# RWKV directions: four elementwise products moved from VectorE to GpSimd between its score factors

## The reference, cut to what matters

```python
a = sigmoid(a0[d] + ad @ a_up[d])
k_d = k * (1.0 + (a - 1.0) * k_a)          # the key of this direction
dirs.append((decay, k_d, a * kk))          # a * kk: rate times key
...
bonus = sum(r * (k_f + k_b) * r_k) * v     # needs the keys of both directions
...
s = s * w_t - (s @ kk_t) ak_t + v_t k_t    # one step of the state, per token
y = s @ r_t
```

## Time and profile before

| | us |
|---|---|
| median of 3 runs | 2219.52 (2217.44 to 2220.51) |
| the profiled execution, its own time | 2221.07 |
| its span | 2219.3 |
| busy TensorE, VectorE, ScalarE, GpSimd | 2041.2, 898.2, 492.2, 103.5 |
| direction 0, rates / decays / scores begin, block ends | 1343.0 / 1359.8 / 1366.7 / 1403 |
| direction 1, the same | 1491.0 / 1508.7 / 1515.6 / 1550 |

### The profile page before, as it was taken

One profiled execution on the slowest core, in us unless ns is written; L12 is line 12 of the kernel. 1 busy time (PEld: TensorE's weight loads), 2 busy tenths in 40 slices (PEclk: granted clock), 3 DMA queues, 4 the chain that ended last, 5 costly groups with the idle time before them and its releaser, 6 DMA issues. The chain is left out here.

```text
span 2219.3 us, 29442 instructions
## 1 busy us (share of the span) xinstructions
PE 2041.2 (92%) x12268; PEld 1209.4 (54%) x12268; DVE 898.2 (40%) x1894; ACT 492.2 (22%) x987; POOL 103.5 (5%) x127
## 2 busy tenths in 40 slices
PE   8999999989999999999998898897977999999994
PEld 3445665536576334585684465783854555544452
DVE  6671064423452112458414677738554221111112
ACT  1000162141122002352023255225212011100001
POOL 0000000002220000000000001302200000000001
PEclk9999999999899999999999998899788999999997
DMA  4222200210001863111121000000027999999995
GB/s 162 76 76 76 76 20 29 68 48 29 29 31 34 341 247 124 57 63 42 39 105 70 26 23 29 2 16 15 2 95 306 414 424 425 424 424 424 424 426 214
DMA packets 54517, 330.35 MB, mean 149 GB/s; under 512 B 6512, under 2 KB 11248, under 8 KB 36080
## 3 DMA queue, kind: packets, MB, share of 16 engines
q1 hardware_dynamic: 53232, 324.26, 37.0%
q0 software_dynamic: 1152, 4.19, 0.5%
HBM read 311.65 MB, written 14.68 MB: 147 GB/s over the span
## 5 line engine op out<-in xcount | busy, mean ns | idle before, releaser
L3514 PE MATMUL psum<-m_ring,m_xg 128*64 128x512 f32 x1024 | 227.9, 600 | 16.9 <-issue 15.8
L246 PE MATMUL psum<-h,wring 128*128 128x512 f32 (+1 forms) x416 | 166.9, 549 | 9.9 <-PEq L93 4.8
L552 PE MATMUL psum<-x,wring 128*128 128x512 f32 x384 | 167.0, 597 | 7.0 <-DVE x L370 7.0
L3514 PEld LDWEIGHTS psum<-m_ring,m_xg 128*64 128x64 f32 x1024 | 77.5, 138 | 164.1 <-issue 162.8
L552 PEld LDWEIGHTS psum<-x,wring 128*128 128x128 f32 x384 | 73.5, 192 | 99.4 <-issue 90.9
L3499 PEld LDWEIGHTS psum<-m_sel,m_htok 128*128 128x128 f32 x1024 | 119.5, 196 | 13.7 <-issue 12.2
L3499 PE MATMUL psum<-m_sel,m_htok 128*128 128x128 f32 x1024 | 123.8, 280 | 1.4 <-DVE m_sel L3490 1.4
L246 PEld LDWEIGHTS psum<-h,wring 128*128 128x128 f32 x416 | 78.3, 195 | 76.8 <-issue 65.0
L3539 PE MATMUL psum<-m_ring,m_hid_t 128*64 128x512 f32 x512 | 115.0, 602 | 0.7 <-ACT m_hid_t L3642 0.7
L3524 DVE TENSOR_TENSOR m_hid<-rstd,psum 64x512 f32<-64x512 f32 x32 | 22.1, 691 | 229.9 <-ACT rstd L3520 229.9
L2056 PE MATMUL psum<-h,wring 128*128 128x512 f32 x192 | 89.5, 623 | 0.9 <-PEq L93 0.7
(11 more groups left out here) (612 smaller groups left out, 3137.3 us busy)
## 6 DMA issues: line engine op xcount, KB each, us to landing
m_ring<-in_w_gate SPq DMA_DIRECT2D x32, 2048.0 KB, 25.7
m_ring<-in_w_up SPq DMA_DIRECT2D x32, 2048.0 KB, 28.0
m_ring<-in_w_down SPq DMA_DIRECT2D x64, 1024.0 KB, 25.5
wring<-in_w1f SPq DMA_DIRECT2D x60, 512.0 KB, 3.3
ada_ring<-in_w_ada SPq DMA_DIRECT2D x12, 2048.0 KB, 10.5
wring<-in_w2f SPq DMA_DIRECT2D x31, 512.0 KB, 3.3
expert_rows<-tmp SPq DMA_DIRECT2D x16, 512.0 KB, 25.9
wring<-in_w1v SPq DMA_DIRECT2D x12, 512.0 KB, 3.2
```

What stands on the lines that cost most here:

```text
L246: return nc.tensor.matmul(place(t, out), lhs, rhs, start=(k == 0), stop=(k == KD - 1))
L552: m = nc.tensor.matmul(K.psum[:, banks[t % 4]], ws.weights(first + t, k), h[:, k], start=(k == 0), stop=(k == KD - 1))
L3514: m = nc.tensor.matmul(K.psum[i * SLOTS:(i + 1) * SLOTS, UP + s], W.xg[:, k, s], w[:, k], start=(k == 0), stop=(k == KD - 1))
```

## The change

Four products per direction go from VectorE to GpSimd. `ak` times `kk` becomes the only GpSimd instruction of the rates (after both halves of `kd`, semaphore `keyed`), so that GpSimd joins the handover `ended`. `bonus` becomes the first GpSimd instruction of the decays and waits for nothing but the handover. `kke` times `kk` is made by GpSimd in two halves of 768 elements, one ahead of its factors of chunk 2 and one ahead of those of chunk 3, and `re` times `r_` (1024 elements) ahead of those of chunk 4. The two products that make `kd` lose their link on VectorE. No transfer is added or moved, and the order of what stays on VectorE, ScalarE and TensorE is the same.

```diff
         for m in range(2):
             eng.wait_ge(sem["sig"], 3 + m)
             link(nc.vector.tensor_scalar(kd[:, m], ak[:, m], -1.0, K.rw[:, 6 + m:7 + m], ALU.add, ALU.mult))
-            link(nc.vector.scalar_tensor_tensor(kd[:, m], kd[:, m], 1.0, k_[:, m], ALU.add, ALU.mult))
-        link(nc.vector.tensor_tensor(ak[:], ak[:], kk[:], ALU.mult))
-        if d == 0:
-            nc.vector.tensor_copy(bonus[:], kd[:, :, CTX:])
-        else:
-            nc.vector.tensor_tensor(bonus[:], bonus[:], kd[:, :, CTX:], ALU.add)
+            nc.vector.scalar_tensor_tensor(kd[:, m], kd[:, m], 1.0, k_[:, m], ALU.add, ALU.mult).then_inc(sem["keyed"], 1)
...
+    def gpsimd(eng, sem):
+        yield 0.6
+        eng.wait_ge(sem["keyed"], 2)
+        nc.gpsimd.tensor_tensor(ak[:], ak[:], kk[:], ALU.mult)
...
-        eng.wait_ge(sem["exped"], 1)
-        nc.vector.tensor_tensor(kke[:], kk[:], kke[:], ALU.mult)
         eng.wait_ge(sem["exped"], 2)
         nc.vector.tensor_tensor(ko[:, 0], kd[:], lw[:], ALU.mult).then_inc(sem["scaled"], 1)
         nc.vector.tensor_tensor(ko[:, 1], ak[:], lw[:], ALU.mult).then_inc(sem["scaled"], 1)
-        eng.wait_ge(sem["exped"], 4)
-        nc.vector.tensor_tensor(re[:], r_[:, :, CTX:], re[:], ALU.mult)
...
     def gpsimd(eng, sem):
+        yield 0.0
+        if d == 0:
+            nc.gpsimd.tensor_copy(bonus[:], kd[:, :, CTX:])
+        else:
+            nc.gpsimd.tensor_tensor(bonus[:], bonus[:], kd[:, :, CTX:], ALU.add)
         yield share
         eng.wait_ge(sem["scaled"], 2)
-        for at_ in scores.engines["gpsimd"](eng, sem):
+        for n, at_ in enumerate(scores.engines["gpsimd"](eng, sem)):
+            if n in (2, 3):
+                m = n - 2
+                eng.wait_ge(sem["exped"], 1)
+                nc.gpsimd.tensor_tensor(kke[:, m], kk[:, m], kke[:, m], ALU.mult)
+            if n == 4:
+                eng.wait_ge(sem["exped"], 4)
+                nc.gpsimd.tensor_tensor(re[:], r_[:, :, CTX:], re[:], ALU.mult)
             yield share + (1 - share) * at_
```

More of the change, by code:

```diff
@@ L2739, in rwkv_direction @@
             (15, rwkv_rates(nc, K, d, up_w, p_mix, kk, k_, kd, ak, lw, ci, ce, e_tot, bias, bonus, range(4))),
-            (54, rwkv_decays(nc, K, kk, r_, kd, ak, lw, ci, ce, at, kke, koT, re, e_tot, range(6),
+            (54, rwkv_decays(nc, K, d, bonus, kk, r_, kd, ak, lw, ci, ce, at, kke, koT, re, e_tot, range(6),
                              rwkv_scores(nc, K, d, r_, kk, kd, ak, both, bias, at, bt, cd, (lw[:], p_mix[:, 4:6]), p_mix[:, 8], range(6)))))
@@ L2811, in vector, with rwkv_decays @@
             nc.vector.tensor_scalar(bias[:, x, :, 2 * NCH:3 * NCH], edge, rate, None, ALU.mult)
-    return Program(["up", "sig", "v"], tensor=tensor, scalar=scalar, vector=vector)
-def rwkv_decays(nc, K, kk, r_, kd, ak, lw, ci, ce, at, kke, koT, re, e_tot, banks, scores):
+    def gpsimd(eng, sem):
+        yield 0.6
+        eng.wait_ge(sem["keyed"], 2)
+        nc.gpsimd.tensor_tensor(ak[:], ak[:], kk[:], ALU.mult)
+    return Program(["up", "sig", "keyed", "v"], tensor=tensor, scalar=scalar, vector=vector, gpsimd=gpsimd)
+def rwkv_decays(nc, K, d, bonus, kk, r_, kd, ak, lw, ci, ce, at, kke, koT, re, e_tot, banks, scores):
     share = 12 / 54
```

## The result

The changed kernel takes 2225.03 us as the median of 12 runs (2220.28 to 2230.53), the kernel before beside it 2218.24 (12 runs): ratio 1.0034 with a 95% interval of 1.0022 to 1.0047, so 7.5 us slower (4.9 to 10.4). One run of the repetition in experiment 8 took 5544.59 us and is left out of its ratio; every other run here lies between 2203 and 2231 us.

What follows compares the result with a forecast made beforehand. The prediction took TensorE as busy for most of the span, with VectorE counting where TensorE waits, in the two RWKV blocks. Rates, decays and scores summed to 4.4 us on the median 2219.5: 2223.9, range 2218.5 to 2229 (forecast's own 2222 to 2226).

Steps and rivals of the forecast that it cites:

- Whole holds: Both blocks: VectorE products with both inputs in SBUF and GpSimd products take turns, whole instruction by whole instruction.
- the turn goes back: Second rival, chance 0.15: VectorE never waits more than 0.54 us within a long GpSimd instruction; about +2 us, 2221.5.
- no contest: Third rival, chance 0.12: a GpSimd product does not hold VectorE up at all; 4.7 us faster, 2214.8.
- Who has the first turn: End of rates and start of decays: GpSimd's start-up of 0.14 us before its first read gives VectorE the turn.
- 1379.3: Score-part collision in direction 0, cited against the first rival: VectorE, started 0.05 us ahead on the same release, went first.
- the first rival: Chance 0.13: GpSimd has the first turn in rates and decays; 3.4 us more, 7.8 us in all, 2227.3.
- rates: Block head up to the handover, with GpSimd's `ak` product: 0.4 us later in direction 0, 0.1 in direction 1.
- decays: Stage after the handover: GpSimd's bonus costs nothing in direction 0; its addition makes L2829 0.5 us later in direction 1.
- Scores: Second half of `kke` and chunk 3's factors delay VectorE's query products: 2.0 us in direction 0, 1.35 in direction 1.
- the ring: Score-part waits: VectorE's mask, ScalarE's corner copy and next query side, VectorE's factors for TensorE; lateness lasts to block end.
- Nothing gained: Taking `kke` and `re` off VectorE gives nothing: VectorE would wait there for an exponential and for TensorE's transposes.
- The sum: 0.4 + 2.0 in direction 0, 0.1 + 0.5 + 1.35 in direction 1: 4.4 us (4.35) slower; forecast chance 0.60.

Runs made afterwards that it cites:

- experiment 8: Kernel before with the bonus alone on GpSimd, behind all factors, where VectorE has only masks left; 2211.34 us, ratio 0.9976, at the repetition 0.9997.
- experiment 2: Kernel before with the bonus alone moved to GpSimd, first in the decays; ratio 0.9991 (0.9975 to 1.0007).
- experiment 3: Kernel before with only `kke` and `re` on GpSimd, between its score factors; 2221.95 us, ratio 1.0017 (1.0006 to 1.0028).
- experiment 7: Changed kernel with the bonus on GpSimd replaced by a memset that reads nothing; VectorE's difference took 1.76 us, no run time given.
- experiment 4: Changed kernel with a small GpSimd memset ahead of the `ak` product and of the bonus; 2218.39 us, ratio 0.9998 to the kernel before.
- experiment 1: Kernel before with only the rate-times-key product (`ak` times `kk`) on GpSimd; 2217.68 us, ratio 0.9995 (0.9985 to 1.0005).

## Why the prediction was right, and what was wrong in it

**Whole holds.** Right. A VectorE product with both inputs in SBUF waits for the rest of a GpSimd product of up to 3.43 us: it was held for 3.25 us, where the forecast's rows showed 0.54. The second and third rivals (the turn goes back, no contest) have fallen. The Trainium skill, "SBUF — State Buffer", section "Who interferes with whom", says that an instruction of VectorE with two SBUF inputs contends with a GpSimd instruction that reads SBUF and not with one that only writes it; the traces agree: products of VectorE took 4.21 us in the changed kernel, 3.96 in experiment 2 and 1.45 in experiment 3, and in experiment 7 one took its bare 1.76.

**Who has the first turn.** This step failed. The forecast said that GpSimd's start-up of 0.14 us keeps it from reading and so gives VectorE the turn. At the four places where it mattered GpSimd's record begins 0.01 to 0.04 us ahead of VectorE's, and GpSimd went first (4.21, 2.62, 4.19 and 3.96 us on VectorE); the 0.59 us after VectorE's end only says how much of a GpSimd product is left once it may read. At 1379.3, which the forecast took as evidence, VectorE's record begins 0.05 us ahead. Where VectorE's instruction before had ended by the time its product started, as at all these places and in experiment 4, the product whose record begins first had the turn.

Where VectorE works without a gap that does not hold. The kernel before, direction 1, and the changed kernel, direction 1:

```profile
1519.96 0.28 DVE L3139 TENSOR_TENSOR p_mix<-r_kk,p_mix 128x128 f32<-128x128 f32 x1
1520.14 1.03 POOL L3179 TENSOR_TENSOR r_lw<-r_kd,p_mix 128x256 f32<-128x256 f32 x1 [2.45 <-ACT p_mix L3097]
1520.16 0.42 DVE L3134 TENSOR_TENSOR r_lw<-r_ak,p_mix 128x256 f32<-128x256 f32 x1
```

```profile
1529.28 1.27 POOL L3187 TENSOR_TENSOR r_lw<-r_kd,p_mix 128x256 f32<-128x256 f32 x1 [2.69 <-ACT p_mix L3105]
1529.34 0.41 DVE L3142 TENSOR_TENSOR r_lw<-r_ak,p_mix 128x256 f32<-128x256 f32 x1
1529.67 0.28 DVE L3143 TENSOR_TENSOR r_lw<-r_ak,p_mix 128x128 f32<-128x128 f32 x1
```

In the first, GpSimd's record begins 0.02 us ahead, and yet L3134, which follows L3139 without a gap, has its bare length, and GpSimd ends 0.59 us behind it. The same stands in the fourteen profiles wherever GpSimd is ahead by 0.02 us or less of a product that follows another VectorE instruction so (37 times). In the second GpSimd is 0.06 to 0.07 us ahead and waits for two products; as far ahead in the second profile of the changed kernel (1380.81) it went first. What decides there is not known. The forecast's reading that GpSimd has its turn between two VectorE instructions that follow without a gap holds for the row that it names (1379.62) and not for these.

What came in place of the forecast's step was the first rival, priced at 3.4 us more. Its parts: rates 0.73 in direction 0 (forecast 0.4, rival 0.8) and 0.05 in direction 1 (0.1, 0.3); decays 0.82 and 2.18 (0 and 0.5; rival 1.0 and 2.3). Experiment 4, which adds two memsets of 0.12 us and so changes the start order, brings the decays to the forecast's figures (0 and 0.5) and the rates to 0.2 and -0.1. The measured 7.5 us are nearer to the rival's 7.8 than to the forecast's 4.35, and the time lies in the range because the range was drawn to hold the rival as well; in that much the forecast was lucky.

**Scores.** The mechanism was right, with the sizes 1.4 to 2.0 in direction 0 (forecast 2.0) and 1.8 to 2.1 in direction 1 (1.35), of which the ring has 1.8 in each. In direction 1 the forecast let chunk 3 meet only one of VectorE's products; both its instructions fell between them, as in direction 0. `re` is covered when the ring is late and costs 1.4 to 1.9 us when it is not (forecast 1.2). The first half of `kke` costs nothing that the ring shows: in direction 0 of experiment 3 it puts the query product of chunk 1 off by 1.6 us, and the first corner copy stands 6.46 us behind the first factor, as before.

**Nothing gained.** Right: with `kke` and `re` gone from VectorE the way to `ko` is 3.31 instead of 3.35 us and the stretch behind it is unchanged (experiment 3).

**The sum.** Rates 0.8, decays 3.0, scores 3.5 or 3.8 (first and second pair of profiles): 7.3 or 7.6 us, against 7.5 measured and 4.35 forecast. Of the 2.9 to 3.3 us that the forecast lacked, some 2.8 are the first turn (rates 0.3, decays 2.5). TensorE's clock added 0.8 us in the first pair of profiles and nothing in the second (-0.1).

**What stays open.** That the whole loss is in the blocks rests on single profiles. The runs of the kernels of experiments 1, 2 and 4 are 1 to 5 us better than their blocks: by their ratios the three parts of the change make -1.1, -2.0 and +3.8 us, together 0.7, where the change makes 7.5, and experiment 4 stands 8 us below the changed kernel, where its blocks account for about 3. Over the 35 runs of the kernel before beside them the time goes with the mean granted clock of the execution, some 1.2 us for 0.001 (correlation -0.61), and these three kernels had 0.9502 to 0.9505 on average against 0.9489, which would be 1.5 to 1.9 us; the runs of the changed kernel and of experiment 3 had 0.9482 and 0.9478, which would be 0.7 and 1.2 us the other way. Why, and whether that is an effect of where the blocks stand in time, was not tried. Nor is it known what makes the transposes of direction 1 meet the lower clock: they did in two of three profiles in which the difference was held for 2.2 us and in none of the eleven others.

## What to carry to other kernels

Before work is moved to GpSimd, look at what VectorE does at the same moment: if it works on two inputs in SBUF, or copies from SBUF to SBUF, the work is not beside it but in line with it, and at half the speed, so a long GpSimd product costs more than it relieves. Put such products where VectorE reads PSUM (masks, evacuations), as the bonus in experiment 8, and, where VectorE is idle and both are released by the same event, look at the start order to the hundredth of a microsecond. Freeing an engine of work that stood in the shadow of another wait gains nothing. A loss of this size also needs its parts read from the timeline and from more than one profile, since TensorE's clock alone moved one stretch from 6.96 to 9.5 us.

## What the runs showed of the hardware

- A copy of six elements on VectorE from SBUF to SBUF is held like a product with two inputs: 3.40 us in experiment 1, 3.27 in experiment 4, by itself 0.17.
- Instructions of VectorE that follow without a gap don't always keep the turn. In most collisions GpSimd and VectorE took turns one for one (1.45, 0.28, 0.94 and 0.54 us in four products that followed each other), but a GpSimd product whose record began 0.02 us ahead of VectorE's next one waited for that too (1.03 us at 1520.14), and one waited for two (1.27 us at 1529.28, its bare length being 0.73).
- GpSimd's product of 1536 elements took 3.43 us, of 1024 2.36, the copy of 1024 1.04, a memset of 1024 0.95; the line through 256 and 512 elements had given 3.43 and 2.35, and half of the copy of 2048 about 1.0.
